# A linear-attention trunk layer: merge gates of six of eight feature pairs as seven half-size products

## What is computed

```python
h = rms_norm(x, norm_w[l]) * (1.0 + scale[:, None]) + shift[:, None]
p = h @ w_in[l]
gq, gk, gv, gz, glr, hq, hf, hi, hz, mg = jnp.split(p, IN_SPLITS, axis=-1)
...
g_a, g_b = jnp.split(jax.nn.sigmoid(mg + merge_b[l]), 2, axis=-1)
m = g_a * (o_g @ w_up_gla[l]) + g_b * (o_h @ w_up_hgrn[l])
x = x + gate[:, None] * (m @ w_out[l])
return rms_norm(x, final_norm_w)
```

## Time and profile before

| | |
|---|---|
| median of 3 runs | 2838.88 us (2838.64 to 2839.45) |
| the profiled execution | 2838.43 us, its span 2836.6 us |
| PE busy | 2797.2 us, 99% of the span |
| DVE / ACT / POOL busy | 44% / 36% / 10% |
| one block in the steady part (400.24 to 746.80 us) | 346.56 us |

### The profile page before, as it was taken

How to read it: one execution, slowest core, us unless ns; L and a number is a source line. 1 busy time by engine, 2 the same in 40 slices (tenths; PEclk the granted TensorE clock), 3 DMA queues, 4 the chain that set the end, 5 groups by cost and what they waited for, 6 DMA issues and landing times.

```text
span 2836.6 us, 35194 instructions
## 1 busy us (share of the span) xinstructions
PE 2797.2 (99%) x14328; PEld 2296.2 (81%) x14328; DVE 1258.9 (44%) x1779; ACT 1023.2 (36%) x1420; POOL 297.1 (10%) x415
## 2 busy tenths in 40 slices
PE   7999999999999999999999999999999999999998
PEld 4878888888887888878888888888888888888886
DVE  7765373432634235342453515525164251633416
ACT  3633345222452134521345213442134421443213
POOL 1441100111001010010100110001100011000101
PEclk9999999999999999999999999999999999999999
DMA  9987865455754557545575466654666546665454
GB/s 372 345 326 248 318 236 205 164 180 206 261 180 164 192 197 261 187 152 205 208 249 179 149 220 216 227 180 148 223 221 227 178 152 221 220 224 178 149 193 163
DMA packets 164129, 604.43 MB, mean 213 GB/s; under 512 B 18496, under 2 KB 18752, under 8 KB 162432
## 3 DMA queue, kind: packets, MB, share of 16 engines
...
q10 hardware_dynamic: 256, 0.20, 0.0%
...
## 4 chain that ended last, share of the span: by engine, by line
PE 97%; DVE 1%; DMA 1%; issue 0%; ACT 0%; SPq 0%; POOL 0%; POOLq 0%; DVEq 0%; ACTq 0%
PE F L1278 33%; PE A L1267 32%; PE A L1332 12%; PE A L1354 9%; PE F L1267 3%; PE F L1354 2%; PE R L1384 1%; PE F L1411 1%; PE A L1426 1%; PE F L1405 1%; DMA ada_w<-in_ada 1%; PE R L1377 1%; DVE h_tmp L873 0%; DVE gates L1030 0%; PE R L1216 0%
## 5 line engine op out<-in xcount | busy, mean ns | idle before, releaser
L1278 PE MATMUL F<-h_hi,w_hi 128*128 128x512 f32 x1408 | 553.9, 393 | 0.0
L1278 PE MATMUL F<-h_lo,w_hi 128*128 128x512 f32 x1408 | 548.2, 389 | 0.0
L1278 PE MATMUL F<-h_hi,w_lo 128*128 128x512 f32 x1408 | 548.2, 389 | 0.0
L1267 PE MATMUL A<-w_hi,h_hi 128*128 128x512 f32 (+1 forms) x1408 | 532.8, 378 | 0.0
L1267 PE MATMUL A<-w_lo,h_hi 128*128 128x512 f32 (+1 forms) x1408 | 523.2, 372 | 0.0
L1267 PE MATMUL A<-w_hi,h_lo 128*128 128x512 f32 (+1 forms) x1408 | 523.0, 371 | 0.0
L1030 DVE TENSOR_TENSOR gates<-gates,A 128x512 f32<-128x512 f32 x128 | 82.3, 684 | 543.5 <-PE A L1332 543.5
L866 DVE TENSOR_TENSOR w_lo<-w_raw,w_hi 128x1024 fp32r<-128x1024 f32 x185 | 242.4, 1311 | 160.8 <-ACT w_hi L619 160.3
L1278 PEld LDWEIGHTS F<-h_hi,w_hi 128*128 128x128 f32 x1408 | 264.3, 188 | 56.3 <-issue 1.7
L1267 PEld LDWEIGHTS A<-w_hi,h_hi 128*128 128x128 f32 x1408 | 264.5, 188 | 55.7 <-issue 8.8
L1278 PEld LDWEIGHTS F<-h_hi,w_lo 128*128 128x128 f32 x1408 | 264.3, 188 | 55.5
...
## 6 DMA issues: line engine op xcount, KB each, us to landing
w_hi<-halves SPq DMA_DIRECT2D x329, 512.0 KB, 3.6
w_lo<-halves SPq DMA_DIRECT2D x329, 512.0 KB, 4.5
w_raw<-pieces SPq DMA_DIRECT2D x112, 512.0 KB, 4.9
w_raw<-in_w_stream SPq DMA_DIRECT2D x71, 512.0 KB, 5.3
halves<-w_hi SPq DMA_DIRECT2D x47, 512.0 KB, 3.3
halves<-w_lo SPq DMA_DIRECT2D x47, 512.0 KB, 4.5
xy<-in_x SPq DMA_DIRECT2D x32, 512.0 KB, 6.2
result<-xy SPq DMA_DIRECT2D x32, 512.0 KB, 7.9
```

What stands on the lines that cost most here:

```text
L1267: last = mm(banks[t][:, 0:width], src[ia][:, k, t * P:(t + 1) * P], w_[iw][:, s % RING, kk * width:(kk + 1) * width], start=(k == 0 and n ...
L1278: last = mm(dst[:, :], w_[iw][:, s % RING, k * P:(k + 1) * P], h_[ia][:, k, :], start=(k == 0 and n == 0), stop=(k == KT - 1 and n == 2))
```

## The change

In blocks 1 to 7 the merge gates of tiles 2 to 7 are made in three groups (`SEVEN`, p = 1, 2, 3), each for a pair of tiles, ja = 2p and jb = 2p + 1, and both gates. Cut by k (`f`, 2 halves), by tile (2) and by tokens (256 early, 256 late) the pair's product is a 2x2 by 2x2 block product, and it is made from seven half-size products in place of eight. Products 0, 1 and 5 take a plain quarter of the weights; 2, 3, 4 and 6 take a sum of weight quarters (`m_pieces`, made once by POOL in block 0, `merge_pieces`). Products 0, 1 and 2 take a plain quarter of h; 3, 4, 5 and 6 take S1, S2, S4 and S3, sums and differences of h quarters (`h_sums`). A product slot is 24 matmuls of 128x256 for both gates. A group is 7 product slots and then the 2 up slots of the pair, where before there were 4 gate slots and 2 up slots. Tiles 0 and 1 (slots 28 to 31), and all of block 0, keep the old form; block 0 leaves the extra slots empty. A block has 75 slot numbers now (`OUT0` = 61).

The results are put together outside PE: ACT copies four partial results out of PSUM (`merge_out`, 128x256, two gates each), DVE adds four (`merge_adds`), ACT applies the sigmoids from `gates` at the group's end. PE may write a bank again, or go on accumulating in it, when such a copy or add is done (`m_cp`, `m_add`). The four weight sums of a group come raw and are split by ACT and DVE again in every block; the three plain quarters come from `halves` in rows of 2 KB where a full slot has rows of 4 KB. The h sums and their split (`S_hi`, `S_lo`) are made once a block, in slots 30 to 36, on DVE and ACT. The split of m tile 5 waits until slot 59, since its buffer holds S4. The four squares of the next block's statistics move to slots 8 to 11 in blocks 1 to 6, with a load of all four x tiles at slot 5.

```diff
-        UP_SLOT[_s] = _j - 1
-        _s += 1
-UP_SLOT[_s] = KT - 1
-_s += 1
-OUT0 = _s
+PAIR_AT = [28, 34, 43, 52]
+UP_SLOT = {32: 0, 33: 1, 41: 2, 42: 3, 50: 4, 51: 5, 59: 6, 60: 7}
+MG_SLOT = {28: (0, 0), 29: (0, 1), 30: (1, 0), 31: (1, 1)}
+SEVEN = {}
+for _p in range(1, 4):
+    for _i, _at in enumerate((0, 2, 3, 5)):
+        MG_SLOT[PAIR_AT[_p] + _at] = (2 * _p + _i // 2, _i % 2)
+    for _n in range(7):
+        SEVEN[PAIR_AT[_p] + _n] = (_p, _n)
+OUT0 = 61
 SLOTS = OUT0 + 14
...
 OG_AT = [24, 24, 25, 26, 28, 28, 29, 29]
 OT_AT = [28, 28, 28, 28, 29, 29, 30, 30]
-XSQ_AT = [40, 40, 43, 44]
-XR_AT = 48
-X_SCALE_AT = [49, 60, 65, 65]
...
+
+        S_hi = [m_unit(1, 6), m_unit(1, 7), h_quarter(h_hi, 0, 1), h_quarter(h_lo, 0, 1)]
+        m_b = [sb(f"m_b{i}", [P, 2, 512], fp32, at=m_at + at) for i, at in enumerate((8192, 12288, 24576, 28672))]
         oraw_at = here()
         o_tm = sb("o_tm", [P, NT, 2 * 512], fp32)
...
+        def mg_banks(p, g):
+
+            return (F[0], F[1], A[0]) if g == 0 else (A[2], A[3], A[1]) if p == 3 else (R[0], R[1], A[1])
...
-                src = pieces[s - OUT0, :, :] if s >= OUT0 else w_stream[s, :, 0:slot_width(s)]
+                b = USES[u][0]
+                if s >= OUT0:
+                    src = pieces[s - OUT0, :, :]
+                elif seven(b, s):
+                    p, n = SEVEN[s]
+                    src = m_pieces[4 * (p - 1) + T_OF[n], :, :]
+                else:
+                    src = w_stream[s, :, 0:slot_width(s)]
                 sp.dma_start(w_raw[:, r, 0:slot_width(s)], src).then_inc(raw_in[r], 16)
 
...
+                        at = PAIR_AT[p] + (3 if product == 5 else 0) - RING
+                        f = 0 if product == 0 else 1
+                        sp.dma_start(part[:, s % RING, 0:1024].bitcast(fp32).rearrange("p (g n) -> p g n", g=2),
+                                     halves[at:at + 3:2, i, :, 512 * f:512 * f + 512]
+                                     .rearrange("g p n -> p g n")).then_inc(halves_in[s % RING], 16)
+                    else:
+                        sp.dma_start(part[:, s % RING, 0:n].bitcast(fp32),
+                                     halves[s - RING, i, :, 0:n]).then_inc(halves_in[s % RING], 16)
...
-                            sp.wait_ge(x_sq.sem, x_sq.at(b + 1, t - 1))
-                            load_x(b + 1, t)
-                    if s + early in (50, 51) and not last:
-                        sp.wait_ge(x_sq.sem, x_sq.at(b + 1, s + early - 47))
-                        load_pair(b + 1, s + early - 50)
-                    if s in (54, 65) and not last:
...
+            def merge_pieces():
+
+                G = nc.gpsimd.tensor_tensor
+                pool.wait_ge(slot_done, DONE[0, 28])
+                for p in range(1, 4):
+                    for i, (to, f) in enumerate(((0, 0), (3, 0), (0, 1), (3, 1))):
+                        if p > 1:
+                            pool.wait_ge(m_b_out[i], 16 * (p - 1))
+                        at = PAIR_AT[p] + to
+                        pool.dma_start(m_b[i][:, :, :], w_stream[at:at + 3:2, :, 512 * f:512 * f + 512]
+                                       .rearrange("g p n -> p g n")).then_inc(m_b_in[i], 16)
+                    for n, (to, x0, x1, piece) in enumerate(((0, 1, 0, 1), (1, 3, 1, 3), (3, 3, 0, 2), (2, 2, 3, 0))):
+                        for i in (0, 1) if n == 0 else (3,) if n == 1 else (2,) if n == 3 else ():
+                            pool.wait_ge(m_b_in[i], 16 * p)
+                        if n:
+                            pool.wait_ge(m_b_link, 4 * (p - 1) + n)
+                        G(m_b[to][:, :, :], m_b[x0][:, :, :], m_b[x1][:, :, :], ALU.subtract).then_inc(m_b_link, 1)
+                        pool.wait_ge(m_b_link, 4 * (p - 1) + n + 1)
+                        pool.dma_start(m_pieces[4 * (p - 1) + piece, :, :].rearrange("p (g n) -> p g n", g=2),
+                                       m_b[to][:, :, :]).then_inc(m_b_out[to], 16)
 
             m_link = signal("m_link", 9)
 
...
                 if first:
                     out_pieces()
+                elif not last:
+                    for t in range(NT):
+                        x_tile(b + 1, t)
                 for i in range(8):
...
                     inverse_root(rstd[:, fam, 4 * t:4 * t + 4], ssq[:, fam, 4 * t:4 * t + 4], rstd_ready)
+                if first:
+                    merge_pieces()
                 m_sums(b, 0)
                 m_sums(b, 1)
-                if not last:
...
+            def merge_out(b, p, n):
+
+                halves_ = slice(0, 256), slice(256, 512)
+                ja, jb, c0 = 0, 1, 4 * (p - 1)
+                if n == 1:
+                    act.wait_ge(up_used.sem, up_used.at(b, 2 * p))
+                for at, (j, late, y) in {1: (ja, 0, 1), 2: (ja, 1, 2), 3: (jb, 1, 1), 4: (jb, 0, 0)}.items():
+                    if n == at:
+                        for g in range(2):
+                            last = AF(gates[:, j, g, halves_[late]], mg_banks(p, g)[y][:, 0:256], ACT.Copy)
+                        last.then_inc(m_cp.sem, 1)
+                if n == 6:
+                    for j in range(2):
+                        act.wait_ge(m_add.sem, m_add.at(b, c0 + 3 + j))
+                        for g in range(2):
+                            feat = g * KT + FEAT[2 * p + j]
+                            AF(gates[:, j, g, :], gates[:, j, g, :], ACT.Sigmoid,
+                               bias=merge_b[:, feat:feat + 1]).then_inc(mg_used.sem, 1)
 
...
+            def merge_adds(b, p, n):
+
+                c0 = 4 * (p - 1)
+                for at, after, j, late, y in ((1, 1, 0, 0, 0), (5, 4, 1, 0, 1), (6, 4, 0, 1, 0), (6, 4, 1, 1, 0)):
+                    if n == at:
+                        dve.wait_ge(m_cp.sem, m_cp.at(b, c0 + after))
+                        for g in range(2):
+                            part = gates[:, j, g, 256 * late:256 * late + 256]
+                            last = V.tensor_tensor(part, part, mg_banks(p, g)[y][:, 0:256], ALU.add)
+                        last.then_inc(m_add.sem, 1)
+
+            def h_sums(b, s):
+
+                TT = V.tensor_tensor
+                if s in (30, 31):
+                    for i, f, late in ((S2, 0, 0), (S3, 0, 1)) if s == 30 else ((S1, 1, 1), (S4, 1, 0)):
+                        TT(S_raw[i], h_quarter(h_hi, f, late).bitcast(fp32), h_quarter(h_lo, f, late).bitcast(fp32),
+                           ALU.add).then_inc(hs.sem, 1)
+                for at, n, to, x0, x1, op in ((32, 4, S1, S1, S3, ALU.add), (32, 5, S3, S2, S3, ALU.subtract),
+                                              (33, 6, S2, S1, S2, ALU.subtract), (33, 7, S4, S4, S2, ALU.subtract)):
+                    if s == at:
+                        dve.wait_ge(hs.sem, hs.at(b, n))
+                        TT(S_raw[to], S_raw[x0], S_raw[x1], op).then_inc(hs.sem, 1)
+                for n, (i, at) in enumerate(((S1, 34), (S2, 35), (S4, 36), (S3, 36))):
+                    if s == at:
+                        dve.wait_ge(hs_hi.sem, hs_hi.at(b, n + 1))
+                        TT(S_lo[i], S_raw[i], S_hi[i].bitcast(fp32), ALU.subtract).then_inc(hs_lo.sem, 1)
+
...
+            def merge_seven(b, s, p, n):
+
+                c0 = 4 * (p - 1)
+                if n == 0:
+                    if p == 1:
+                        pe.wait_ge(mg_used.sem, mg_used.at(b, 4))
+                    else:
+                        pe.wait_ge(m_add.sem, m_add.at(b, c0))
+                if n == 2:
+                    pe.wait_ge(up_used.sem, up_used.at(b, 2 * p - 1))
+                if n == 4:
+                    pe.wait_ge(m_add.sem, m_add.at(b, c0 + 1))
+                if n in (3, 5, 6):
+                    pe.wait_ge(m_cp.sem, m_cp.at(b, c0 + {3: 1, 5: 3, 6: 4}[n]))
+                of_h = {0: (0, 0), 1: (1, 0), 2: (1, 1)}
+                of_s = {3: S1, 4: S2, 5: S4, 6: S3}
+                if n in of_s:
+                    pe.wait_ge(hs_lo.sem, hs_lo.at(b, of_s[n] + 1))
+                    src = S_hi[of_s[n]], S_lo[of_s[n]]
+                else:
+                    src = h_quarter(h_hi, *of_h[n]), h_quarter(h_lo, *of_h[n])
+                for g in range(2):
+                    if p == 3 and n == 0 and g == 1:
+                        pe.wait_ge(up_used.sem, up_used.at(b, 6))
+                    dst = mg_banks(p, g)[(0, 1, 2, 1, 0, 1, 0)[n]][:, 0:256]
+                    for kk in range(4):
+                        for i, (iw, ia) in enumerate(PASSES):
+                            last = mm(dst, w_[iw][:, s % RING, 512 * g + kk * P:512 * g + (kk + 1) * P],
+                                      src[ia][:, kk // 2, kk % 2, :], start=(n < 4 and kk == 0 and i == 0),
+                                      stop=(kk == 3 and i == 2), skip_group_check=True)
+                last.then_inc(slot_done, 1)
 
```

(18 more changed lines are left out.)

167 lines of the change are left out of this document (116 added, 51 removed).

## The result

The changed kernel takes 2851.93 us (median of 5 runs, 2847.21 to 2852.72), the kernel before, measured beside it, 2838.64 (2835.99 to 2839.45). The ratio is 1.0047, interval 1.0034 to 1.006: it is slower by 0.3 to 0.6%, where the forecast was 2833.6, a little faster. The profiled execution took 2852.72 us, span 2850.9. (The "six of eight feature pairs" of the title are six of the eight feature tiles, tiles 2 to 7, taken in three pairs.)

What follows compares the result with a forecast made beforehand. PE, busy 99% of the span, sets the pace. 39.0 us saved, less 7 x (3.7 + 0.9) = 32.2 and 1.5, leaves 5.3: 2833.1 us for the profiled execution, 2833.6 for the median; range 2810 to 2860.

Steps and rivals of the forecast that it cites:

- What the products save: Gates of blocks 1 to 7: 256-column matmuls 118.5 ns apart, 5.6 us saved a block, 39.0 over seven.
- the bracket of 117.5 to 119.4: Spacing in ns of 256-column matmuls on PE, from two trace rows; saves 6.1 to 5.1 us a block.
- the 98 interpolated from them: Spacing in ns at 256 columns by the skill's figures; by it the products would lose 82 us over seven blocks.
- Group 1's h sums: DVE alternates with POOL; slots 37 and 38 wait 2.7 and 0.95 us, 3.7 a block.
- Group 3's bank: Slot 52: gate 1 writes A2, still used by slot 51's up product; PE waits 0.9 us a block.
- Other handovers, squares, 2 KB rows: Handovers in groups, squares in slots 8 to 11, product 5's loads: covered, nothing taken; 2 KB rows at worst 25 us.
- Block 0's pieces: POOL's three rounds end at 326 us, may push to 335; ACT may stand until 329: 0 to 6 us, 1.5 taken.
- ACT's copy: Rival: copy behind product 3 or another handover misses by half a us or more in 21 groups; 2850 us, chance 0.11.
- Block 0's pieces 8 to 15 us late: Rival: the pieces in block 0 come 8 to 15 us late; 2845 us, chance 0.07.

Runs made afterwards that it cites:

- The four counters: The kernel before, with `pieces_out` as four semaphores, one for each buffer, instead of one for all: 2833.76 us, ratio 0.9985.

## Why the prediction was wrong

The direction was wrong, by 19.6 us in the profiled execution. That 2851.93 still lies within the stated 2810 to 2860 is luck: the two steps that cost most of the miss, the output stage and block 0's weight buffers, have no part in how that range was made. By its steps:

- **What the products save.** Right in kind, 5.4 us too much: "I take 118.5" should have been 120 (the slot of 2.88), within the bracket of 117.5 to 119.4 but for 0.6. The Trainium skill (TensorE: Matmul & The Clock Gate, Back-to-back issue gap) gives sustained spacings of about 81 ns at 128 columns and 131 at 512; the 98 interpolated from them is contradicted by these 120, as is 131 by 226.7.
- **Group 1's h sums.** The mechanism was right, shown by moving POOL away. The size was 4.0 us too large in all: each turn of the two engines costs 1.68 us and not 1.22 + 0.74, so slot 37 starts 1.97 late and not 2.7, and slot 38 0.6 and not 0.95. At the 2.6 us of the blocks with full clock it would be 7.4 too large; the halved clock, which the forecast does not have, gave 3.4 back.
- **Group 3's bank.** Right: 0.92 for 0.9, shown by the other bank.
- **Other handovers, squares, 2 KB rows.** Right within some 3 us: beside slots 36 to 38 and 52 the product slots lose 2.9 us in all, slots 0 to 31 of blocks 1 to 7 last as before (to 0.01 us). For `halves` PE waits once, 0.2 us, in the product slots, which alone load rows of 2 KB, and 1.4 us in all in the up slots, whose rows are whole.
- **The step that failed: the output stage was never costed.** The change moves tile 5's split to slot 59, and the text counts it nowhere. The section on the kernel before gives every slot 24 matmuls; output slots have 12 and last 2.72 us, so DVE has half the time there that a gate slot gives. Late by 1.7 us at slot 60, it cost 10.8 us over eight blocks (with block 0's 2.0), and moving the split back took 8.0 of them off. That alone turns 5.3 us saved into a loss.
- **Block 0's pieces.** "I take 1.5" was mis-sized, and its place was wrong. The chain of POOL's rounds ended before ACT asked for it: its last store landed at 316.6 us (forecast 326), and ACT split tile 4 at 331.1. The stall came some 25 us before that, from POOL's and SP's transfers together (382 GB/s for 298 in that stretch) on a buffer order with one slot of lead. It measured 8.7 us, 2.9 of them by the halved clock.
- **A gain not seen.** The four counters were in the diff, and the 6.0 us "issue" in the earlier trace rows; it was not followed to its cause. It is worth 4.6 us alone; in the changed kernel slots 20 to 23 are 3.0 shorter.

The four misses: +5.4, -4.0, +10.8 and +7.2 (block 0), less 3.0 and with 3.2 of small waits, make 19.6. Of the rivals, ACT's copy, at 2850, is nearest in number and did not happen: no product slot waits for ACT. "Block 0's pieces 8 to 15 us late" has about the size of block 0's loss, by another mechanism.
